# Two attention layers: where the local queries are transposed, the order of turns and value products, and which engine makes the low parts of four weight units

## The reference, cut to what matters

```python
a_z, bq, bk, bv, cq, ck, cv = split_proj(h @ w_in[i])        # and the same of hc for the context
out_a = chunk_gmlp(a_z, a_ws[i], a_bs[i])                     # A: GELU, norm of the values, 128-token mixing
q_b = apply_rope(rms_norm(bq..., b_qnorm[i]), cos_b, sin_b)   # B, local: 8 heads of 64, 2 key heads,
out_b = window_attn_latent(q_b, k_b, v_b, k_bc, v_bc, b_sink[i])   # window of 128, the context, and a sink
q_c = rope_maps(rms_norm(cq..., c_qnorm[i]), cos_c, sin_c)    # C, differential: 4 heads, 2 maps of 32,
o_c = diff_attn_latent(q_c, k_c, v_c, k_cc, v_cc, lam)        # (softmax_0 - lam * softmax_1) @ v
out_c = rms_norm(o_c, c_subln[i]) * (1 - lam_init)
x = x + g1 * (concatenate([out_a, out_b, out_c]) @ w_out[i])
x = x + g2 * conv_ffn(modulate(rms_norm(x, norm2_g[i]), sh2, sc2), ...)
...
```

## Time and profile before

| | |
|---|---|
| median of 3 runs | 1831.83 us (1831.83, 1830.77, 1834.18) |
| the profiled execution | 1828.93 us, of which the span in the profile is 1827.1 us |
| TensorE busy | 1741.1 us, 95% of the span |
| VectorE busy | 1031.6 us |
| ScalarE busy | 860.9 us |
| GpSimd busy | 358.7 us |
| TensorE's granted clock, mean | 0.983 of full |

### The profile page before, as it was taken

One profiled execution on the slowest core, in us unless ns is written; L12 is line 12 of the kernel. 1 busy time (PEld: TensorE's weight loads), 2 busy tenths in 40 slices (PEclk: granted clock), 3 DMA queues, 4 the chain that ended last, 5 costly groups with the idle time before them and its releaser, 6 DMA issues.

```text
span 1827.1 us, 30029 instructions
## 1 busy us (share of the span) xinstructions
PE 1741.1 (95%) x12614; PEld 1563.2 (86%) x12614; DVE 1031.6 (56%) x1804; ACT 860.9 (47%) x1290; POOL 358.7 (20%) x220
## 2 busy tenths in 40 slices
PE   6999989999999999999988999999999898799999
PEld 6999878898999999998866878777888787599999
DVE  2377469687775885267763175413552377538840
ACT  4432545447445665445654253313432356556653
POOL 4301540000000115700001301132114200041147
PEclk9999989999999999999999999999999899989999
DMA  6643535544565554431100422154223222035544
GB/s 263 221 194 149 198 142 206 201 166 186 208 237 224 186 185 143 159 120 47 69 1 4 175 89 96 64 195 175 96 90 125 80 89 93 1 116 185 185 153 147
DMA packets 40967, 258.76 MB, mean 142 GB/s; under 512 B 4352, under 2 KB 7552, under 8 KB 14464
## 3 DMA queue, kind: packets, MB, share of 16 engines
q1 hardware_dynamic: 40832, 256.84, 38.3%
HBM read 255.77 MB, written 1.05 MB: 141 GB/s over the span
## 4 chain that ended last, share of the span: by engine, by line
PE 85%; DVE 10%; ACT 3%; issue 1%; POOL 1%; DMA 0%; SPq 0%; DVEq 0%; ACTq 0%
PE acc_psum L194 23%; PE acc_psum L196 23%; PE acc_psum L195 22%; PE acc_psum L2246 3%; PE acc_psum L235 2%; PE acc_psum L2202 2%; PE acc_psum L319 2%; PE acc_psum L923 2%; DVE w_low_sb L160 1%; PE acc_psum L2225 1%; PE acc_psum L254 1%; DVE norm_sq_sb L579 1%; DVE norm_rt_sb L1575 1%; ACT w_high_sb L149 1%; PE acc_psum L1217 0%
## 5 line engine op out<-in xcount | busy, mean ns | idle before, releaser
L194 PE MATMUL acc_psum<-h_high_sb,w_high_sb 128*128 128x256 f32 (+1 forms) x2144 | 665.4, 310 | 10.9 <-DVE h_low_sb L388 4.6
L196 PE MATMUL acc_psum<-h_high_sb,w_low_sb 128*128 128x256 f32 (+1 forms) x2144 | 657.8, 307 | 0.0
L195 PE MATMUL acc_psum<-h_low_sb,w_high_sb 128*128 128x256 f32 (+1 forms) x2144 | 657.7, 307 | 0.0
L149 ACT ACTIVATE w_high_sb<-ring_sb 128x1024 fp32r<-128x1024 f32 (+2 forms) x412 | 386.5, 987 | 456.7 <-PE acc_psum L196 244.7
L194 PEld LDWEIGHTS acc_psum<-h_high_sb,w_high_sb 128*128 128x128 f32 x2144 | 411.1, 192 | 41.2 <-issue 18.8
L160 POOL TENSOR_TENSOR w_low_sb<-ring_sb,w_high_sb 128x1024 fp32r<-128x1024 f32 (+2 forms) x150 | 297.5, 2007 | 683.8 <-ACT w_high_sb L149 683.8
L195 PEld LDWEIGHTS acc_psum<-h_low_sb,w_high_sb 128*128 128x128 f32 x2144 | 410.4, 191 | 18.9 <-issue 0.5
L196 PEld LDWEIGHTS acc_psum<-h_high_sb,w_low_sb 128*128 128x128 f32 x2144 | 410.4, 191 | 18.6
L160 DVE TENSOR_TENSOR w_low_sb<-ring_sb,w_high_sb 128x1024 fp32r<-128x1024 f32 (+1 forms) x262 | 306.4, 1211 | 55.6 <-ACT w_high_sb L149 46.2
L1796 DVE SCALAR_TENSOR_TENSOR u_filtered<-acc_psum,par_sb,u_filtered 128x255 f32<-128x255 f32 (+2 forms) x264 | 150.9, 572 | 153.5 <-ACT u_filtered L1903 141.2
L1931 POOL TENSOR_TENSOR u_low<-u_filtered,u_high 128x256 fp32r<-128x256 f32 (+1 forms) x66 | 61.1, 926 | 778.4 <-ACT u_high L1924 778.4
(11 more groups left out here) (296 smaller groups left out, 2015.7 us busy)
## 6 DMA issues: line engine op xcount, KB each, us to landing
ring_sb<-in_w_in SPq DMA_DIRECT2D x68, 1024.0 KB, 6.5
ring_sb<-in_w_up SPq DMA_DIRECT2D x66, 1024.0 KB, 4.8
ring_sb<-in_w_ada SPq DMA_DIRECT2D x48, 1024.0 KB, 4.8
ring_sb<-in_w_down SPq DMA_DIRECT2D x48, 704.0 KB, 4.1
ring_sb<-in_w_out SPq DMA_DIRECT2D x12, 1024.0 KB, 5.6
ring_sb<-in_w_br_hg SPq DMA_DIRECT2D x4, 1024.0 KB, 6.9
ring_sb<-in_w_br_ml SPq DMA_DIRECT2D x4, 1024.0 KB, 7.0
ring_sb<-in_w_br_mb SPq DMA_DIRECT2D x4, 1024.0 KB, 8.2
```

Source lines behind the costliest of these rows:

```text
L149: self.nc.scalar.activation(self.high[:, g % 2, piece], self.ring[:, c % RING, piece], ACT.Copy)\
L194: nc.tensor.matmul(out, sh, mh, start=start, stop=False)
L195: nc.tensor.matmul(out, sh, ml, start=False, stop=False)
L196: return nc.tensor.matmul(out, sl, mh, start=False, stop=stop)
```

## The change

It has four parts.

1. `GAP` is 2 in layer 0 and 3 in layer 1, and steps may now run in the last slots past `B0`: in layer 0 the scores of the first two B units go into the last slot, in layer 1 those of the first.
2. So the B queries and keys have to be transposed earlier. `turn_b` is in two parts: keys and queries of heads 0 to 2 into banks 2 to 5, behind the last group of the slot before the last (layer 0) or behind the first group of the last slot (layer 1), and queries of head 3 into bank 6, behind the second group of the last slot. The copies of the transposed tiles move from the tail's start into the last slot, on ScalarE and VectorE. The step of C's last norm on VectorE (the reciprocal of `subs`) moves two steps back.
3. In `second_part` the second turn of a unit stands ahead of the value product of the unit before.
4. The last four units of `w_in_2` of each layer in the order of the stream (2, 3, 1, 0) get their low parts from GpSimd, no longer from VectorE.

```diff
-        def add(name, idx, low, first, rides=()):
+        def add(name, idx, low, first, rides=(), late=None):
             for i, n in enumerate(idx):
-                stream.append((a[name][n], low if i else first))
+                stream.append((a[name][n], first if i == 0 else late if late and i >= 4 else low))
...
-            add("w_in_2", [8 * i + n for n in (6, 5, 7, 4, 2, 3, 1, 0)], "dve", "pool")
+            add("w_in_2", [8 * i + n for n in (6, 5, 7, 4, 2, 3, 1, 0)], "dve", "pool", late="pool")
...
-    GAP = 4
+    GAP = 3 if last else 2
+    TURNED = (4, 0, 1, 2, 3)
...
-        return [st for st in (2 * (s - S0), 2 * (s - S0) + 1) if 0 <= st < B0 and s < NS]
-    TAIL = range(B0, U + 4)
+        return [st for st in (2 * (s - S0), 2 * (s - S0) + 1) if st >= 0 and s < NS]
+    TAIL = range(2 * (NS - S0), U + 4)
...
                 if u in (B0, B0 + 1):
+                    pe.wait_ge(*tu_act.at(4))
+                    pe.wait_ge(*tu_dve.at(4))
+                if u == B0 + 3:
                     pe.wait_ge(*tu_act.at(5))
-                    pe.wait_ge(*tu_dve.at(4))
...
+                if u == B0:
+                    pe.wait_ge(*tu_act.at(5))
                 for m in (0,) if kind == "C" else (second,) if long(u) else (0, 1):
...
             def second_part(st):
+                if real(st - 2):
+                    turn(st - 2, 1)
                 if real(st - 3):
                     values(st - 3)
-                if real(st - 2):
-                    turn(st - 2, 1)
...
-            def turn_b():
-                pe.wait_ge(*prep_b.at(1))
-                pe.wait_ge(*exr.at(NC))
-                pe.wait_ge(*tbc.at(NC))
-                for j in range(5):
+            def turn_b(part):
+                if part == 0:
+                    pe.wait_ge(*prep_b.at(1))
+                    pe.wait_ge(*exr.at(NC))
+                else:
+                    pe.wait_ge(*tbc.at(NC))
+                for n in range(4) if part == 0 else (4,):
+                    j = TURNED[n]
...
-                if s == NS - 1 and q == 3:
-                    turn_b()
+                if (s, q) == ((NS - 1, 0) if last else (NS - 2, 3)):
+                    turn_b(0)
+                if s == NS - 1 and q == 1:
+                    turn_b(1)
...
+            def turned_b(part):
+                for n in part:
+                    n_ = (NT if n == 0 else NQ) * P
+                    act.wait_ge(*tu.at(4 + n + 1))
+                    nc.scalar.activation(TT[:, TURNED[n], 0:n_], psum[:, 2 + n, 0:n_], ACT.Copy).then_inc(*tu_act.one())
...
+                if s == NS - 1:
+                    turned_b((0, 2))
                 steps = steps_in(s)
                 for st in steps[:1]:
                     step(st)
...
                 for st in steps[1:]:
                     step(st)
+                if s == NS - 1:
+                    turned_b((4,))
...
+        @block.gpsimd
+        def _(pool):
+            for g in range(2, len(ORDER) + 1):
+                core.split_low(pool, g0 + g, "pool")
...
             for st in TAIL:
-                if st == TAIL[0]:
-                    for j in (2, 3):
-                        dve.wait_ge(*tu.at(4 + j + 1))
-                        nc.vector.tensor_copy(TT[:, j, 0:T], psum[:, 2 + j, 0:T]).then_inc(*tu_dve.one())
                 step(st)
                 if st == TAIL[0]:
                     spatial_values()
+                if st == TAIL[2]:
                     dve.wait_ge(*sub_s.at(1))
                     link(nc.vector.reciprocal(subs[:, 0:NQ, :], subs[:, 0:NQ, :]))
```

12 lines of the change are left out of this document (6 added, 6 removed).

## The result

The changed kernel took 1844.22 us (median of 6 runs, 1841.32 to 1849.16) against 1833.01 us for the kernel before in the same comparison (6 runs, 1828.67 to 1835.9): a ratio of 1.006, 95% interval 1.0044 to 1.0076. That is 11.2 us slower, where 5.6 was forecast. The two profiled executions are further apart: 17.2 us, a span of 1844.3 against the 1827.1 of the earlier trace rows. The one of the kernel before ran 4.1 us under its median, the one of the changed kernel 1.9 over its own.

A forecast was written before the change was run, and what follows sets the result against it. TensorE, busy 95% of the 1827.1 us span, bounds the kernel. Slots +8.6, tails -7.8 and clock +4.8 give +5.6: 1834.5 from the profiled 1828.9, 1837.4 against the median; 8-in-10 range 1826 to 1845.

The forecast's parts named there:

- the three places named: Slots: TensorE waits over 3 us at the first layer's third and fourth moved units and the second layer's third.
- The slots: Attention work between projection groups: GpSimd low parts block VectorE's two-SBUF-input instructions, costing 8.6 us over both layers.
- The tails: Attention-only ends of both layers: earlier scores and reordered turns gain 6.3 us in the first, 1.5 in the second.
- The step that moves the scores: First tail's start: transposes and two score pairs move into the last slots, bringing k2's first turn 5.1 us earlier.
- one of my own signs of being wrong: First tail: k2's (third local-attention unit's) turn more than 2 us off 10.4 behind the last product.
- The step on the order of turns: Tails: second turn ahead of values hides copy waits; first layer's k2 to k8 takes 27.0 us against 28.4.
- +0.8 us: Whole kernel before clock effects: slots +8.6 and tails -7.8 together.
- three drops of 1.6, +4.8 us: TensorE's clock falls behind three of four longer idle stretches, each costing 1.6 us; bounds nothing to 12.
- the rows from 930 on: Kernel before, first tail: clock averaged 0.55 and 0.59 of full from 930 to 934, used to price each drop.
- The clock holds: Rival: no clock drops behind the new waits, +0.8 to +3 us, 1832.6 to 1835; 30%.
- GpSimd doesn't hold VectorE: Rival: small two-input instructions pass GpSimd's pieces, slots lose nothing, 9.6 us less, 1822.3; 12%.
- Low clock lasts twice as long: Part of the rival that more than one place is worse, 1841 to 1847; 13%.

The follow-up runs named there:

- e7: Kernel before, with GpSimd making the low parts of only the first two of the four units per layer: 1833.79 us against 1833.09, ratio 1.0008.
- e3: Kernel before, with only the second turn put ahead of the previous unit's value product: 1823.41 us against 1833.91, ratio 0.9953.
- e1: Kernel before, with only the low parts of four units per layer given to GpSimd: 1847.17 us against 1833.91, ratio 1.0074.
- e2: Changed kernel without the GpSimd low parts, both tails changed: 1832.76 us against 1833.91 for the kernel before, ratio 1.0001.
- e5: Changed kernel without GpSimd low parts, ScalarE's two roots moved into the last slot: 1825.8 us against 1833.66 for the kernel before, ratio 0.9955.
- e11: e5 with the early transposes and scores in the first layer only: 1824.35 us against 1833.09 for the kernel before, ratio 0.9959.

## Why the prediction was right, and where it was off

**Direction, range and mechanism** came out: slower, inside 1826 to 1845, with VectorE instructions held up at the three places named. The size did not: 11.2 us, twice the 5.6 of the sum, above the 1835 to 1841 that the forecast itself gave and only 0.8 us under the upper bound. That the range held is partly luck.

**The slots.** 8.6 us were forecast, 6.6 in the first layer and 2.0 in the second. TensorE's idle time in the slots grew by 5.2 and 1.6 us. The three waits are 3.19, 3.46 and 3.18 us, each 0.1 to 0.5 under the forecast, and the further 0.9 us given to the turn behind the fourth unit's value product did not come: that turn, at 902.13, does not wait. That one VectorE instruction gets through between two pieces was met to the letter (2.12 and 2.18 us). That the first two units of a layer cost nothing is shown by e7.

**The tails.** 7.8 us were forecast, 6.3 and 1.5; idle time in them fell by 3.9 and 2.4. The step that moves the scores (5.1 us at the start) failed: k2's turn came 12.7 us behind the last product, not 10.4, 2.3 off, and over 2 was one of my own signs of being wrong. The waits in it were right. TensorE's rows:

```profile
941.86 1.09 PE L2233 MATMUL acc_psum<-con_sb,norm_rt_sb 128*128 128x128 f32 x4 [2.68 <-ACT arena_attention L2468]
942.88 2.08 PE L2207 MATMUL acc_psum<-arena_attention 64*128 64x512 f32 x4
...
948.04 0.61 PE L2233 MATMUL acc_psum<-con_sb,norm_rt_sb 128*128 128x128 f32 x4
```

k1's turn comes 6.5 us behind the last product (6.4 forecast). From it to k2's turn it is 6.2 us where I had 3.95, since the turns and scores take nearly twice their time: the clock is at half from 940 to 947. By itself this part made the kernel 11.2 us slower, where I had expected 4 us faster. The step on the order of turns came out: k2's to k8's turn took 26.2 us (948.04 to 974.27) against 27.0 forecast and 28.4 before, in steps of 4.74, 4.26 and 4.1 where I had 4.9, 4.4 and 4.2. For e3, the same step alone, I had only carried its 1.4 us over; there no side product stands in these steps, and it gave 4.1. The waits of slots and tails together rose by 0.5 us, against the "+0.8 us" of the sum.

**The clock** is the term that was mis-sized: "three drops of 1.6, +4.8 us". The runs of the parts say where. e1, the slots' part alone, cost 13.3 us, and 8.6 plus 4.8 are 13.4. It is near by some luck, since its waits were shorter than forecast and the drops behind them longer (3.4, 3.4 and 1.7 us of TensorE's time). e2, the tails' part alone, was to gain 7.8 us and gained nothing (1.0001), with 6.8 us less of waiting. So what the sum lacks most is the clock lost with the changed tails.

In the changed kernel's trace all four stretches were followed by a drop. TensorE's busy time times one minus the clock, summed over the windows of low clock, is 1.7 and 1.5 us in the first layer's slots, 2.8 in the second's and 4.2 at the second tail, 10.2 together. More drops stood behind waits of 1.8, 1.6 and 2.5 us of the second layer that I had not counted (1499, 1554 and 1564), though the kernel before waits 1.8, 2.4 and 2.2 us at these places and kept full clock in its first trace, and in the first tail 2.5 us were lost where the earlier trace rows have 1.7. The upper bound in the text, 12 us if all drop and stay low for some 6 us, was nearer than the value taken. I chose the rows from 930 on because they stand in the same code; those at 1600, also in a tail, had lasted twice as long. Of the 17 us that the traces show, 11 are in the medians: both traces of the kernel before were executions 4 to 5 us under its median, with fewer drops than most. Why the clock falls behind one wait and not behind an equal one stays open.

**The rivals.** "The clock holds" fell: all six runs of the changed kernel have a mean clock of 0.969 to 0.972. "GpSimd doesn't hold VectorE" fell at 871.73. "Low clock lasts twice as long", the third rival, is what happened in the second tail, and 1844.2 lies in its 1841 to 1847, to which I had given 13%.

**What beats both kernels**: the new order of turns alone (e3, 1823.4 us, 0.9953), and with the earlier scores and the roots moved (e5, e11) about the same. I tried no version with GpSimd's low parts on top of these.

## What to carry to other kernels

Split a trace into TensorE's busy and idle time before explaining a difference: if the busy time grew with the same instructions by more than the last section's 1 to 2 us, look at the clock first, and the question is which waits came just before the low stretches. Give a new wait of some 3 us on TensorE a price for the clock too (the four here, 14.0 us, lost another 10.2 to it), read from several traces and not from one; waits that are not new can be followed by low clock as well. Before work is moved to GpSimd, look at which VectorE instructions with two SBUF inputs stand beside it, and whether TensorE is due behind them; their number of columns did not matter here (2.18 and 2.12 us for one and two columns, 2.46 for 256).
